# Conditioning of the first feed-forward layer as rows instead of columns, inside the RWKV loop of a two-layer encoder

## What is computed

```python
mod = jax.nn.silu(c) @ w + b                    # c: (1, 2048), w: (2048, 6144), four of them
shift, scale, gate = jnp.split(mod[:, None, :], 3, axis=-1)
h = x * (1.0 + scale) + shift                   # x: (1, 256, 2048)
z = h @ w_in                                    # layer 0: RWKV-7 (16 heads of 64) and GLA (4 heads) side by side
x = _layer_norm(ALPHA * x + (1.0 + gate) * f(h), ln_g, ln_b)
```

## Time and profile before

| | us |
|---|---|
| median of 3 runs | 2932.14 (2922.16 to 2932.91) |
| the profiled execution | 2923.16 |
| its span | 2920.9 |
| input projection | 50 to 348 |
| prologue (t = -2, -1) | 348 to 406 |
| RWKV loop, t = 0 to 7 | 406 to 794 |
| rest of the second mixer | 794 to 849 |
| output projection | 849 to 945 |

### The profile page before, as it was taken

One profiled execution on the slowest core, in us unless ns is written; L12 is line 12 of the kernel. 1 busy time (PEld: TensorE's weight loads), 2 busy tenths in 40 slices (PEclk: granted clock), 3 DMA queues, 4 the chain that ended last, 5 costly groups with the idle time before them and its releaser, 6 DMA issues. The chain is left out here.

```text
span 2920.9 us, 42283 instructions
## 1 busy us (share of the span) xinstructions
PE 2759.6 (94%) x17774; PEld 2311.4 (79%) x17774; DVE 1943.6 (67%) x1885; ACT 1184.5 (41%) x1373; POOL 271.5 (9%) x199
## 2 busy tenths in 40 slices
PE   3999889999989999999999979999999999999996
PEld 3888788888867788888888868888877888888885
DVE  5778624444558688888888788776477855555557
ACT  2555423333443433333333434546443333333332
POOL 0000000000000400000000019363022000000000
PEclk9999968999899899999999989999999999999998
DMA  8888533332147588888888737664548755555552
GB/s 309 296 293 306 195 95 92 88 86 79 31 176 285 212 312 308 331 306 331 308 312 324 276 115 245 245 232 144 200 164 332 279 191 186 187 190 193 192 187 87
DMA packets 320856, 636.70 MB, mean 218 GB/s; under 512 B 10606, under 2 KB 82980, under 8 KB 304708
## 3 DMA queue, kind: packets, MB, share of 16 engines
q1 hardware_dynamic: 314546, 621.84, 60.8%
q10 hardware_dynamic: 6162, 12.72, 1.2%
HBM read 632.42 MB, written 2.10 MB: 217 GB/s over the span
## 5 line engine op out<-in xcount | busy, mean ns | idle before, releaser
L531 DVE TENSOR_TENSOR s_wl<-s_raw,s_wh 128x2048 fp32r<-128x2048 f32 (+1 forms) x393 | 913.9, 2326 | 516.2 <-ACT s_wh L526 507.1
L526 ACT ACTIVATE s_wh<-s_raw 128x2048 fp32r<-128x2048 f32 x396 | 758.4, 1915 | 1084.6 <-PE pa L726 419.4
L724 PE MATMUL pa<-s_wh,s_hth 128*128 128x512 f32 x1312 | 527.6, 402 | 13.7 <-DVE s_wl L531 8.5
L725 PE MATMUL pa<-s_wl,s_hth 128*128 128x512 f32 x1312 | 517.3, 394 | 0.0
L726 PE MATMUL pa<-s_wh,s_htl 128*128 128x512 f32 x1312 | 516.9, 394 | 0.0
L724 PEld LDWEIGHTS pa<-s_wh,s_hth 128*128 128x128 f32 x1312 | 249.8, 190 | 75.4 <-DVE s_wl L531 13.1
L726 PEld LDWEIGHTS pa<-s_wh,s_htl 128*128 128x128 f32 x1312 | 250.0, 191 | 53.6
L725 PEld LDWEIGHTS pa<-s_wl,s_hth 128*128 128x128 f32 x1312 | 250.3, 191 | 48.7
L724 PE MATMUL pb<-s_wh,s_hth 128*128 128x512 f32 x704 | 274.5, 390 | 0.0
L726 PE MATMUL pb<-s_wh,s_htl 128*128 128x512 f32 x704 | 274.2, 389 | 0.0
L725 PE MATMUL pb<-s_wl,s_hth 128*128 128x512 f32 x704 | 274.2, 389 | 0.0
(11 more groups left out here) (396 smaller groups left out, 3756.3 us busy)
## 6 DMA issues: line engine op xcount, KB each, us to landing
s_raw<-in_ffn_w_in SPq DMA_DIRECT2D x176, 1024.0 KB, 5.3
s_adaw<-in_ada_w SPq DMA_DIRECT2D x144, 1024.0 KB, 6.1
s_raw<-in_ffn_w_out SPq DMA_DIRECT2D x88, 1024.0 KB, 8.1
s_raw<-in_ab_w_in SPq DMA_DIRECT2D x48, 1024.0 KB, 8.8
s_raw<-in_diff_w_in SPq DMA_DIRECT2D x48, 1024.0 KB, 5.2
s_adaw<-in_ada_w SPq DMA_DIRECT2D x48, 512.0 KB, 5.5
s_raw<-in_ab_w_out SPq DMA_DIRECT2D x16, 1024.0 KB, 9.8
s_qkv<-in_ada_w SPq DMA_DIRECT2D x16, 1024.0 KB, 7.2
```

The lines of the kernel that those rows point to most:

```text
L526: act.activation(wh[:, s % 2, :, 0:width], raw[:, s, :, 0:width], ACT.Copy).then_inc(hi_done, 1)
L531: dve.tensor_tensor(wl[:, s % 2, :, 0:width], raw[:, s, :, 0:width], wh[:, s % 2, :, 0:width].bitcast(F32), ALU.subtract).then_inc(lo_done, 1)
L724: pe.matmul(o, a_hi, w_hi, start=start and k == 0, stop=False)
L725: pe.matmul(o, a_hi, w_lo, start=False, stop=False)
```

## The change

The 32 bursts and the eight pairs of the output projection go. In their place:

- Eight pairs more in the input projection. `EARLY` lists 40: the 24 of shift and scale where they were, and the two halves of sub-layer 0's gate, group 4 at units 13, 14, 24, 26, 27, 37, 39 and 40, and group 5 at units 43 to 50 (the one half that was there stood at 40 to 47). Both use the second half of `wide`. Their column sums stand behind units 41 and 51, where one stood behind unit 49.
- 32 row loads for shift and scale of sub-layer 1: `row_load` brings 128 whole rows of 2048 columns (8 KB each).
- `row_products`: for each, four f32 products of 512 columns. The weights are one column of silu(c), repeated 32 times, and product j writes partitions 32 j to 32 j + 31 of one PSUM bank. Sixteen rows are summed up in PSUM.
- after 16 rows `rows_copy` (ScalarE) copies the bank, `rows_turn` (TensorE) transposes it, `rows_store` (VectorE) adds the bias. This happens in t = 2 and t = 7.
- `ROWS_IN` gives 2 and 6 rows in t = -2 and -1, at their end, 4 in t = 0, 1, 3, 4 and 5, and 2 in t = 2 and 6. In a pass of four, three stand in levels 2 to 4 between the recurrence's product and `level_v`, the fourth at the pass's end.

```diff
-        def burst(pe, b, half):
-
-            n = BURST_LOADS + b
-            if half == 0:
-                pe.wait_ge(*loaded(n))
-            col = BURST[:, half * BURSTS + b:half * BURSTS + b + 1]
-            block = adaw[:, n % 2].rearrange("p (k n) -> p k n", k=KT)
-            for k in range(half * KT // 2, (half + 1) * KT // 2):
-                mm = pe.matmul(col, block[:, k], silu_c[:, k:k + 1], start=(k == half * KT // 2),
-                               stop=(k == (half + 1) * KT // 2 - 1), skip_group_check=True)
-            mm.then_inc(burst_done, 1)
...
+        def row_load(sp, b):
+
             if b < 2:
-                sp.wait_ge(ada_step, JOB_STEPS + 2 * (n - 1))
+                sp.wait_ge(ada_step, JOB_STEPS + 2 * (len(EARLY) + b - 1))
             else:
-                sp.wait_ge(burst_done, 2 * (b - 1))
...
+                sp.wait_ge(rows_done, b - 1)
+            sp.dma_start(adaw[:, b % 2], parts[1, b // KT, b % KT]).then_inc(wide_in[b % 2], 16)
...
+        def row_products(pe, b):
+
+            k = b % KT
+            pe.wait_ge(wide_in[b % 2], EARLY_IN[b % 2] + 16 * (b // 2) + 16)
+            if b == KT:
+                pe.wait_ge(rows_out, 1)
+            for j in range(4):
+                mm = pe.matmul(ROWS[32 * j:32 * j + 32], silu_c[:, k:k + 1].to_broadcast((P, 32)), adaw[:, b % 2, j * W:(j + 1) * W],
+                               start=(k == 0), stop=(k == KT - 1), skip_group_check=True)
+            mm.then_inc(rows_done, 1)
+
+        def rows_copy(act, m):
+
+            act.wait_ge(rows_done, KT * m + KT)
+            act.activation(wide[:, 0:W], ROWS, ACT.Copy).then_inc(rows_copied, 1)
+
+        def rows_turn(pe, m):
+
+            pe.wait_ge(rows_copied, m + 1)
+            for j in range(4):
+                mm = pe.transpose(ROWS[:, j * P:(j + 1) * P], wide[:, j * P:(j + 1) * P], ident)
+            mm.then_inc(rows_turned, 1)
...
-                    bursts(t, 0)
                     level_q(t, 2)
                 if chain:
                     chain_x(c, 1)
                 if lev:
-                    bursts(t, 1)
+                    rows_at(t, 0)
...
-            half_cols(pe, 4, TAIL_STEPS + 2 * PAIR_LOADS)
```

More of the change, by code:

```diff
@@ L306, in build_trunk @@
         JOB_STEPS = 1 + len(JOBS) * 17
[L307 to L318, removed]
+        EARLY = sorted([(ABC * s + 2 + i, s + 1, i) for s in range(3) for i in range(8)]
+                       + [(q, 4, i) for i, q in enumerate((13, 14, 24, 26, 27, 37, 39, 40))]
+                       + [(q, 5, i) for i, q in enumerate(range(43, 51))])
+        EARLY_AT = [q for q, g, i in EARLY]
+        EARLY_IN = [sum(32 if g < 4 else 16 for q, g, i in EARLY[slot::2]) for slot in range(2)]
+        ROW_LOADS = 32
+        ROWS_IN = {-2: 2, -1: 6, 0: 4, 1: 4, 2: 2, 3: 4, 4: 4, 5: 4, 6: 2}
+        PART_STEPS = JOB_STEPS + 2 * len(EARLY) - 48
+        PART_IN = [n + 16 * (ROW_LOADS // 2) - 16 * 24 for n in EARLY_IN]
+        FIRST_JOBS = len(JOBS) + 5 - 3
         const_in = sem("const_in")
@@ L346, in build_trunk @@
         z1_summed = sem("z1_summed")
-        burst_done = sem("burst_done")
-        burst_out = sem("burst_out")
+        rows_done = sem("rows_done")
+        rows_copied = sem("rows_copied")
+        rows_turned = sem("rows_turned")
+        rows_out = sem("rows_out")
         pa_free = sem("pa_free")
@@ L570, in part_step @@
             frm = adaw[:, slot] if frm is None else frm
-            dve.wait_ge(wide_in[slot], half * 16 + (8 * PART_LOADS + 16 + 8 * LATE_LOADS))
+            dve.wait_ge(wide_in[slot], half * 16 + (PART_IN[slot] + 16))
             if isinstance(k, int) and k == 0:
@@ L579, in part_step, with early_step, early_cols @@
                                          ALU.add).then_inc(ada_step, 1)
[L581 to L589, removed]
+        def early_step(dve, n):
+            q, g, i = EARLY[n]
+            dve.wait_ge(wide_in[n % 2], sum(32 if EARLY[m][1] < 4 else 16 for m in range(n % 2, n + 1, 2)))
             for kk in range(2):
-                frm, to, k = adaw[:, n % 2, kk * D // 2:(kk + 1) * D // 2], wide[:, 0:D // 2], 2 * i + kk
+                frm, k = adaw[:, n % 2, kk * D // 2:(kk + 1) * D // 2], 2 * i + kk
+                to = wide[:, 0:D // 2] if g < 4 else wide[:, D // 2:D]
                 if k == 0:
-                    dve.wait_ge(ada_cols, len(JOBS) + (n // PAIR_LOADS if n < BURST_LOADS else 4))
+                    dve.wait_ge(ada_cols, len(JOBS) + {1: 0, 2: 1, 3: 2, 4: 0, 5: 4}[g])
                     dve.tensor_scalar(to, frm, silu_c[:, 0:1], None, ALU.mult).then_inc(ada_step, 1)
                 else:
-                    dve.wait_ge(ada_step, at + kk)
+                    dve.wait_ge(ada_step, JOB_STEPS + 2 * n + kk)
                     dve.scalar_tensor_tensor(to, frm, silu_c[:, k:k + 1], to, ALU.mult, ALU.add).then_inc(ada_step, 1)
[L599 to L604, removed]
+        def early_cols(pe, g):
+            last = max(n for n in range(len(EARLY)) if EARLY[n][1] == g)
+            pe.wait_ge(ada_step, JOB_STEPS + 2 * last + 2)
+            pe.wait_ge(ada_out, len(JOBS) + g - 1)
+            at = 0 if g < 4 else D // 2
+            for j in range(8):
+                mm = pe.matmul(pt[:, 1, j:j + 1], wide[:, at + j * P:at + (j + 1) * P], ones[:, 0:1], start=(j == 0), stop=True,
                                skip_group_check=True)
@@ L1664, in _ @@
                     gla_gate_act()
+                if t in (2, PAIRS - 1):
+                    rows_copy(act, 0 if t == 2 else 1)
                 if lev:
@@ L2767, in gla_turn_out, with rows_at @@
                 mm.then_inc(g_oT, 1)
[L2769 to L2777, removed]
+            def rows_at(t, at):
+                if t not in ROWS_IN:
+                    if t == PAIRS - 1 and at == 1:
+                        rows_turn(pe, 1)
+                    return
+                b = sum(ROWS_IN[i] for i in range(-2, t))
+                if t < 0:
+                    mine = range(ROWS_IN[t]) if at == 3 else ()
+                elif t == 2:
+                    if at == 0:
+                        rows_turn(pe, 0)
+                    mine = (at - 2,) if at >= 2 else ()
                 else:
-                    mine = range(2 * BURSTS_IN[t]) if at == 6 else ()
+                    mine = (at,) if at < ROWS_IN[t] else ()
                 for i in mine:
-                    burst(pe, *halves[first_half + i])
+                    row_products(pe, b + i)
             for t in range(-2, PAIRS + 1):
@@ L2832, in _ @@
                 if lev:
-                    bursts(t, 2)
                     level_q(t, 3)
@@ L2837, in _ @@
                 if lev:
-                    bursts(t, 3)
+                    rows_at(t, 1)
                 if t == PAIRS:
@@ L2861, in _ @@
                 if lev:
-                    bursts(t, 5)
+                    rows_at(t, 2)
                 if lev and not gla:
@@ L2894, in _ @@
                 if t < PAIRS:
-                    bursts(t, 6)
+                    rows_at(t, 3)
                 if front:
```

97 lines of the change are left out of this document (38 added, 59 removed).

## The result

The kernel after takes 2805.48 us (median of four runs, 2805.04 to 2805.83), the kernel before, run beside it, 2932.52 us (2922.16 to 2938.10). The ratio is 0.957, 95% interval 0.954 to 0.960: 4.3% faster. The prediction said 2832 and 2808 to 2872. The profiled execution of after took 2805.04 us, its span is 2803.0.

A forecast was written before the change was run, and what follows sets the result against it. TensorE was taken to bound the loop. Loop -97, prologue -3, input projection +3, output projection -0.3 gave -97 from the profiled 2923.2: 2826, or 2835 as median; 2832 us was said, range 2808 to 2872.

The forecast's parts named there:

- its low clock at the start as now: Pass t = 0: 46.2 us less 16.4 of bursts plus four rows, clock staying low at the start: 33.8 us.
- A row costs 1.0 us, a burst 1.88: Loop: a half burst takes 1.88 us; a row's four products run at once in 1.0; pass t = 5 about 37.0.
- No new waits in the loop, level 4 even: Loop: V waits for nothing at level 2; level 4 even within 0.3 us. Rival of new waits: 2864, chance 0.07.
- The clock would be full without one-column products: Loop: one-column products alone get a low clock; without them t = 1, 3, 4 and 5 take 37.0 us each.
- t = 7 with the mixer, -14.4: Pass t = 7: 53.4 us now, 16.7 of them bursts, at 0.78 of the clock; forecast 39 us.
- allowance of 2.3 us for late gates of the second mixer: Pass t = 7: VectorE's work for the second mixer's gates comes late without bursts, so 39 us, not 36.7.
- Prologue -3: Prologue: two rows replace two halves, 3.3 us less; six rows bound by loads take 18.4 for 18.08; together 3 less.
- a load lands after 5.9 us: Prologue: four of six rows must be loaded into two buffers, each load landing after 5.9 us; 18.4 us in all.
- Input projection +3: Input projection: 16 more VectorE steps cost 0 to 20 us, taken as 1; one more column sum 1.84; together 3 more.
- Behind the mixer -0.3: Output projection: only the store of 0.15 us with its drain leaves the path, 0.3 less.
- From the profiled execution to the median: Total: before's median is 9 us above its profiled execution, making 2826 into 2835; 2832 was said, between the two.
- a way to lose: Rival, loop at the half clock because bursts that filled TensorE's waits go: 90 to 100 us more, 3025; chance 0.07.

The follow-up runs named there:

- rows of one column: The kernel after with 30 of its 32 rows cut to one product of one column in place of four of 512: 2791.09 us.
- before_wide_bursts: The kernel before, each burst product streaming 64 columns in place of one: 2892.67 us, against 2930.31 for the kernel before on the same chip.
- The kernel with both edits: The kernel after with rows moved into TensorE's waits and 4, 5, 5 rows in t = -1, 0, 1: median 2795.46 us, ratio to before 0.954.

## Why the prediction was right or wrong

The mechanism held, the size did not: 2832 was 26.5 us too high. Two steps failed most. The sum kept "its low clock at the start as now" in t = 0 and put 33.8 us on the pass, which took 28.2 at a clock of 0.97. And it added 6 us for the way from the profiled execution to the median, which measured 0.4. The other misses are of about 3 us each.

- **A row costs 1.0 us, a burst 1.88.** Right. The groups of 256 columns in the earlier trace rows gave all three prices to 0.01 us, and the pass at full clock was 36.45 us for 36.9.
- **No new waits in the loop, level 4 even.** Right, and shown by the rows of one column: 0.7 us of wait appears there when the row goes. That a cheaper row "would gain little there" holds for level 4: 3.4 us less of rows made a pass 2.5 shorter, and what is lacking is that wait.
- **The clock would be full without one-column products.** The mechanism is right for the loop, and wide bursts show it alone. Its size was off. The term "t = 0 ... its low clock at the start as now" is the largest miss of a stretch: 33.8 us forecast, 28.2 measured. The rows are not to blame: a fifth row in t = 0 (the kernel with four rows in t = -1) makes the pass 0.9 longer, at the same 0.97. The prediction itself said that one-column products alone get a low clock, and did not apply it to the pass that starts right behind the longest run of bursts.
- **t = 7 with the mixer, -14.4.** Measured -17.5. Wide bursts give 10.6 of these from the clock alone. The allowance of 2.3 us for late gates of the second mixer was not measured by itself; no run separates it from the clock, which was 0.93 over this stretch.
- **Prologue -3.** Measured -5.5. The step that failed is the load: "a load lands after 5.9 us" came from the earlier trace rows, which shows loads in short pieces, while the diff loads rows in one piece per partition. Counted from 347.5 us, the prologue of before lasts 58.4 us, that with rows in short pieces 56.3, near the forecast, and after's 52.9.
- **Input projection +3.** Measured +0.1, the low end of its bounds (0 to 20). Sixteen VectorE steps were hidden altogether: from 50 to 348 us TensorE's waits for the weight splits are 6.2 and 1.6 us in both traces. The last column sum, 1.84 us, stands where the kernel before had a gap of 0.98 us of instruction issue ahead of the next products, and the other stands behind unit 41, where before had one behind unit 49. In after, from 50 to 348 us:

```profile
PE pa L2434 <- DVE s_wl L521: 6.2, 2, 5.1
PE pb L2434 <- DVE s_wl L521: 1.6, 2, 1.1
```

- **Behind the mixer -0.3.** Measured -3.4. In the output projection, up to the first products behind its normalization, it is 1.1 less; the prediction had 0.3 for the removed work. The rest, 2.2 us, is of the size by which the same code differs between kernels (2065.5 to 2072.1 us in the experiments), and no cause is shown.
- **From the profiled execution to the median.** The prediction added 6 us because before's median stood 9 above its profiled execution. After's median stands 0.4 above its profiled execution, so the 6 were an error whole. Before's runs go from 2922 to 2943 us, and the longer ones have the lower clock (2942.87 us at 0.956, 2924.30 at 0.962): its median carries a spread that goes with the clock, and that after would have the same was assumed without a reason. The kernel with both edits spreads too, over 7 us; why after's four runs agree within 0.8 is open.
- **The range.** It names 8 us by which two terms together could come out better, and 12 and 20 for terms that could come out worse; its lower end lies 24 below the forecast, and what the rest of these is the prediction does not say. The clock was named only as a way to lose. The gain's side should have held the clock of t = 0 (5.6) and of the mixer (3.1) as well: 2808 less these is 2799.

The sum: against the profiled execution the terms missed 20.4 us of span (t = 0 5.7, the passes t = 1 to 6 3.1, mixer 3.1, prologue 2.5, input projection 2.9, behind the mixer 3.1), and the step to the median added 6.

## What to carry to other kernels

A product of one column is dearer than its place in the order of time: ask what clock the products around it get, for in this kernel a quarter of the gain (30 of 118 us) was had by letting the same products stream 64 columns. In a product of a matrix with a vector let the matrix be streamed, and load the vector as the weights, repeated over the 32 columns of each column group: 1 MB of the matrix then takes 1.00 us for 3.76. Then put such filler where the engine waits anyway: four full rows cost a pass 2.5 us more than rows of one column where the change put them, and 0.3 to 0.6 in TensorE's waits. In the prologue this is not shown: with the six rows of t = -1 moved too, prologue and t = 0 took 1.7 us more.

## What the runs showed of the hardware that was not expected

- The granted clock is 0.90 in a pass with one-column bursts and 1.00 with bursts of 64 columns, at nearly the same busy share of TensorE (94% and 93%) and nearly the same duration of the burst (1.88 and 1.93 us).
- Four column groups of 512 f32 columns take 1.00 us, two 1.84, one 3.55, between products of 64 by 64 tiles. Entering and leaving cost some 0.1 us of these: a row in four groups is two times 0.453 us from start to start, 0.91, and one in a single group eight times 0.429, 3.43.
- After a wait of 2.4 us for a load the granted clock was 0.50 with TensorE busy 7.04 of 7.10 us and 64 columns streamed; before that wait it was 1.00 with the same products (`before_wide_bursts`).
- A load of 1024 KB, with little else to load, lands after 5.0 us in pieces of 8 KB and after 5.9 in pieces of 512 bytes.
